# A layer stack with routed experts on one core: overflow blocks ahead of expert 28, products of ones during the routing, and up weights in four transfers

## The reference, cut to what matters

```python
def hier_moe(u, ...):                       # u: 264 x 1024
    g_sel = argmax(x @ w_group + b_group)   # one of 4 groups
    vals, idx = top_k(inner logits of that group, 2)
    gate = softmax(vals) * g_w
    expert_id = g_sel * 8 + idx             # two of 32 experts for a token
    return moe_experts(x, expert_id, gate, w1, w3, w2)
...
    hmid = silu(xblk @ w1[e]) * (xblk @ w3[e])    # 1024 -> 512, twice
    return hmid @ w2[e]                           # 512 -> 1024
...
h = h + hier_moe(rmsnorm(h), ...)
h = h + sigmoid(rmsnorm(h) @ w_gate + b_gate) * (p_i @ w_proj)    # ple
```

## Time and profile before

| | us |
|---|---|
| median of 3 runs (1632.49 to 1643.6) | 1632.73 |
| profiled execution, its own time | 1640.69 |
| its span | 1638.9 |
| TensorE busy (mean granted clock 0.835) | 1212.1 |
| DVE busy | 505.1 |
| ACT busy | 264.8 |

### The profile page before, as it was taken

One profiled execution on the slowest core, in us unless ns is written; L12 is line 12 of the kernel. 1 busy time (PEld: TensorE's weight loads), 2 busy tenths in 40 slices (PEclk: granted clock), 3 DMA queues, 4 the chain that ended last, 5 costly groups with the idle time before them and its releaser, 6 DMA issues. The chain is left out here.

```text
span 1638.9 us, 23206 instructions
## 1 busy us (share of the span) xinstructions
PE 1212.1 (74%) x10112; PEld 784.2 (48%) x10112; DVE 505.1 (31%) x1337; ACT 264.8 (16%) x643; POOL 58.9 (4%) x46
## 2 busy tenths in 40 slices
PE   6978697865766756479898897979675776766577
PEld 4846454433433433247675554745443443433355
DVE  2783512112111111143575663141111112111133
ACT  1262221100100000001224431012010000000011
POOL 0430000000000000000200100000000000000000
PEclk9989788877877877769999996959887887787788
DMA  5853259999999999915213432719999999999820
GB/s 158 278 206 133 103 239 419 420 420 422 420 419 422 422 419 419 416 73 174 103 45 137 153 137 103 280 54 381 419 419 423 421 419 419 422 421 419 353 104 27
DMA packets 91279, 477.03 MB, mean 291 GB/s; under 512 B 21676, under 2 KB 32841, under 8 KB 73230
## 3 DMA queue, kind: packets, MB, share of 16 engines
q1 hardware_dynamic: 89188, 456.35, 68.9%
q0 software_dynamic: 1792, 18.88, 3.1%
q10 hardware_dynamic: 186, 0.20, 0.0%
HBM read 473.37 MB, written 2.49 MB: 290 GB/s over the span
## 5 line engine op out<-in xcount | busy, mean ns | idle before, releaser
L878 PE MATMUL ps<-area,hiddenT 128*32 128x256 f32 x2112 | 214.3, 575 | 287.7 <-issue 279.9
L878 PEld LDWEIGHTS ps<-area,hiddenT 128*32 128x32 f32 x2112 | 97.7, 155 | 376.8 <-issue 368.3
L1417 DVE COPY y<-ps 32x256 f32<-32x256 f32 x128 | 53.3, 417 | 534.8 <-PE ps L878 526.3
L868 PE MATMUL ps<-area,uT 128*32 128x256 f32 x2176 | 145.4, 425 | 4.0 <-issue 1.7
L1151 PE MATMUL ps<-sel,u_rows 128*128 128x256 f32 (+3 forms) x480 | 136.9, 417 | 10.4 <-DVE sel L1123 10.4
L868 PE MATMUL ps<-area,xsT 128*32 128x256 f32 x2048 | 131.6, 412 | 0.0
L1371 ACT COPY y<-ps 32x256 f32<-32x256 f32 x128 | 46.7, 365 | 485.1 <-PE ps L878 484.1
L868 PEld LDWEIGHTS ps<-area,uT 128*32 128x32 f32 x2176 | 85.8, 126 | 64.5 <-issue 32.3
L1151 PEld LDWEIGHTS ps<-sel,u_rows 128*128 128x128 f32 (+1 forms) x480 | 85.3, 214 | 55.0 <-issue 49.9
L868 PEld LDWEIGHTS ps<-area,xsT 128*32 128x32 f32 x2048 | 80.2, 123 | 53.4 <-issue 21.9
L1276 PE MATMUL ps<-share,y 128*128 128x264 f32 x256 | 77.5, 429 | 13.7 <-DVE y L1417 9.9
(11 more groups left out here) (324 smaller groups left out, 1260.1 us busy)
## 6 DMA issues: line engine op xcount, KB each, us to landing
area<-in_w_exp_gate_dram SPq DMA_DIRECT2D x66, 2048.0 KB, 27.0
area<-in_w_exp_up_dram SPq DMA_DIRECT2D x66, 2048.0 KB, 30.7
area<-in_w_exp_down_dram SPq DMA_DIRECT2D x66, 2048.0 KB, 26.2
area<-in_conv_w_in_dram SPq DMA_DIRECT2D x8, 1024.0 KB, 12.8
area<-in_w_ple_gate_dram SPq DMA_DIRECT2D x2, 4096.0 KB, 17.8
area<-in_conv_w_out_dram SPq DMA_DIRECT2D x1, 4096.0 KB, 19.2
area<-in_w_o_dram SPq DMA_DIRECT2D x1, 4096.0 KB, 13.2
area<-in_w_uq_dram SPq DMA_DIRECT2D x3, 768.0 KB, 10.1
```

The lines of the kernel that those rows point to most:

```text
L868: last = pe.matmul(s.ps[SLOT * j:SLOT * (j + 1), bank, 0:2 * P].rearrange("p (a f) -> p a f", a=2), xT[:, k, :], up[:, :, k, j * P:(j + 1) ...
L878: last = pe.matmul(s.ps[SLOT * g:SLOT * (g + 1), bank, 0:q], hidden[:, SLOT * j:SLOT * (j + 1)], down[:, j, g * q:(g + 1) * q], start=(j = ...
L1417: last = V.tensor_copy(y[a:a + SLOT, (e // PER) % 2, g * q4:(g + 1) * q4], s.ps[SLOT * g:SLOT * (g + 1), 3 + e % 2, 0:q4])
```

## The change

Overflow blocks run ahead of expert 28 (`CUT`) instead of behind expert 31, on all engines, and are added to the tokens four at a time. The loop of loads is written anew: up to expert 27 its order is as before, and from there on it is up e, down e in place of up e+1, down e. Overflow block q uses the slots of expert 28 + q, so the loads of expert 28 wait for the blocks (`ov.up`, `ov.down`). `PLE_SLOT` becomes 2, the slot of expert 29, and the attention's buffers change rooms accordingly. Eight and twelve products of ones stand on TensorE in the routing (`busy`); their result is not used. Each half of the contraction of gate and up is a transfer of its own, 1 MB each, and a half has its own semaphore, for which TensorE waits in the midst of the up products. The register load of the number of overflow blocks moves from the start of the stage to expert 28.

```diff
-PLE_SLOT = 1
+PLE_SLOT = 2
+CUT = E - PER
...
-def load_up(engine, s, io, slot, index, sem):
+def load_up(engine, s, io, slot, index, sems):
     up = up_view(s, slot)
-    for a, w in enumerate((io["w_exp_gate"], io["w_exp_up"])):
-        src = w.rearrange("l e (p k) f -> (l e) p (k f)", p=P)[bass.ds(index, 1)]
-        engine.dma_start(up[:, a].rearrange("p k f -> p (k f)"), src.rearrange("a p n -> (a p) n"))\
-            .then_inc(sem, 16)
+    for half, sem in enumerate(sems):
+        k = slice(DC // 2 * half, DC // 2 * (half + 1))
+        for a, w in enumerate((io["w_exp_gate"], io["w_exp_up"])):
+            src = w.rearrange("l e (p k) f -> (l e) p k f", p=P)[bass.ds(index, 1), :, k]
+            engine.dma_start(up[:, a, k], src.rearrange("a p k f -> (a p) k f")).then_inc(sem, 16)
...
+        def busy(pe, n):
+            for k in range(n):
+                pe.matmul(s.ps[:, 3, 0:T], s.ones[:], s.uT[:, k % DC, :], start=True, stop=True)
...
+                busy(pe, 8)
                 pe.wait_ge(s.gated.sem, s.gated.at(2))
...
                 pe.wait_ge(s.turned_out_act.sem, on_act)
+                busy(pe, 12)
                 pe.wait_ge(s.sel_ready.sem, s.sel_ready.at(1))
...
+        def blocks_of(engine, n, block, quad_begins=None, quad_ends=None, after=None):
+            def chain(q):
+                with engine.If(n > q):
+                    block(q)
+                    if (q + 1) % PER:
+                        chain(q + 1)
+                    if after is not None:
+                        after(q)
+            def quad(b):
+                with engine.If(n > PER * b):
+                    if quad_begins is not None:
+                        quad_begins(b)
+                    chain(PER * b)
+                    if quad_ends is not None:
+                        quad_ends(b)
+                    if b + 1 < MAX_OVER // PER:
+                        quad(b + 1)
+            quad(0)
...
+                def up(e):
+                    sp.wait_ge(s.up_done.sem, s.up_done.at(e - UPS + 1))
+                    load_up(sp, s, io, e, e + layer * E, [half.sem for half in s.up_in[e % UPS]])
...
+                for e in range(UPS, CUT):
+                    up(e)
+                    down(e - 1)
                 n = overflow(sp)
...
+                with sp.If(n > 0):
+                    more_up(0)
+                down(CUT - 1)
+                blocks_of(sp, n, more, after=lambda q: sp.wait_ge(ov.up, q + 1))
+                up(CUT)
+                blocks_of(sp, n, lambda q: sp.wait_ge(ov.down, q + 1))
+                down(CUT)
+                for e in range(CUT + 1, E):
+                    up(e)
+                    down(e)
+                sp.wait_ge(s.up_done.sem, s.up_done.at(E - UPS + 1))
                 load_ple_gate(sp, s, io, layer)
...
+                def combine_more(b):
+                    pe.wait_ge(ov.g_ready, b + 1)
                     for c in range(DC):
...
+                        pe.matmul(s.ps[:, 6 + c % 2, 0:T], y[:, 1, c * P:(c + 1) * P], more_share[:, 0, :],
                                   start=True, stop=True).then_inc(ov.comb_mm, 1)
...
-                n = overflow(pe)
                 for e in range(E):
...
+                    if e == CUT:
+                        blocks_of(pe, overflow(pe), more, quad_ends=combine_more,
+                                  after=lambda q: pe.wait_ge(ov.y_ready, q + 1))
+                    def ready(k):
+                        if k % (DC // 2) == 0:
+                            half = k // (DC // 2)
+                            pe.wait_ge(s.up_in[e % UPS][half].sem, up_at(e)[half])
...
-                further(pe, more, n)
                 for c in range(DC):
                     combine(quads - 1, c)
```

More of the change, by code:

```diff
@@ L241, in setup_state @@
         ov.sel_half, ov.sel_ready = sem("ov_sel_half", layer), sem("ov_sel_ready", layer)
-        ov.xs_mm, ov.xs_out, ov.g_half = sem("ov_xs_mm", layer), sem("ov_xs_out", layer), sem("ov_g_half", layer)
-        ov.up_in = [sem(f"ov_up_in{i}", layer) for i in range(UPS)]
+        ov.xs_mm, ov.xs_out = sem("ov_xs_mm", layer), sem("ov_xs_out", layer)
+        ov.g_half, ov.g_ready = sem("ov_g_half", layer), sem("ov_g_ready", layer)
+        ov.up_in = [[sem(f"ov_up_in{i}_{half}", layer) for half in range(2)] for i in range(UPS)]
         ov.down_in = [sem(f"ov_down_in{i}", layer) for i in range(DOWNS)]
         s.over_sems.append(ov)
-    s.up_in = [Count(ctx, nc, f"up_in{i}") for i in range(UPS)]
+    s.up_in = [[Count(ctx, nc, f"up_in{i}_{half}") for half in range(2)] for i in range(UPS)]
     s.down_in = [Count(ctx, nc, f"down_in{i}") for i in range(DOWNS)]
@@ L854, in first_up @@
 def first_up(sp, s, io, layer, n):
-    load_up(sp, s, io, n, layer * E + n, s.up_in[n].sem)
+    load_up(sp, s, io, n, layer * E + n, [half.sem for half in s.up_in[n]])
 def first_down(sp, s, io, layer, n):
@@ L929, in _ @@
             def _(sp):
-                first_up(sp, s, io, layer, 2 - layer)
+                first_up(sp, s, io, layer, 2)
             @block.tensor
@@ L1193, in fill_at, with over_xsT @@
             return (i + 1, f) if 0 <= f < pairs else None
+        def over_xsT(g):
+            return xsT[0 if g == GROUPS else 1]
         def up_at(n):
-            return s.up_in[n % UPS].at(32 * (n // UPS + 1))
+            return [half.at(32 * (n // UPS + 1)) for half in s.up_in[n % UPS]]
         def down_at(n):
@@ L1216, in more_up @@
                     if q < UPS:
[L1217 removed]
+                        sp.wait_ge(s.up_done.sem, s.up_done.at(CUT - UPS + q + 1))
                     else:
                         sp.wait_ge(ov.up, q - UPS + 1)
[L1220 removed]
+                    load_up(sp, s, io, CUT + q, e + layer * E, ov.up_in[(CUT + q) % UPS])
                 def more_down(q):
@@ L1234, in more, with down @@
                     more_down(q)
-                n = overflow(sp)
[L1237 to L1256, removed]
+                def up(e):
+                    sp.wait_ge(s.up_done.sem, s.up_done.at(e - UPS + 1))
+                    load_up(sp, s, io, e, e + layer * E, [half.sem for half in s.up_in[e % UPS]])
+                def down(e):
+                    sp.wait_ge(s.down_done.sem, s.down_done.at(e - DOWNS + 1))
+                    load_down(sp, s, io, e, e + layer * E, s.down_in[e % DOWNS].sem)
+                for e in range(UPS, CUT):
+                    up(e)
+                    down(e - 1)
+                n = overflow(sp)
+                with sp.If(n > 0):
[9 more added lines that the diff above has]
+                sp.wait_ge(s.up_done.sem, s.up_done.at(E - UPS + 1))
                 load_ple_gate(sp, s, io, layer)
@@ L1419, in copy_out, with weigh_more @@
                     last.then_inc(s.y_dve.sem, 1)
+                def weigh_more(b):
+                    halves = weigh(nc, m, P, more_share, col(s, "over_of")[:, b:b + 1])
+                    next(halves).then_inc(ov.g_half, 1)
+                    dve.wait_ge(ov.g_half, b + 1)
+                    next(halves).then_inc(ov.g_ready, 1)
                 def more(q):
@@ L1460, in _ @@
                     quad = e // PER
+                    if e == CUT:
+                        blocks_of(dve, overflow(dve), more, weigh_more, add_more)
                     dve.wait_ge(s.acted.sem, s.acted.at(e + 1))
@@ L1483, in experts_stage @@
         for k in range(UPS):
-            s.up_in[k].ended(32 * len(range(k, E, UPS)))
+            for half in s.up_in[k]:
+                half.ended(32 * len(range(k, E, UPS)))
         for k in range(DOWNS):
```

92 lines of the change are left out of this document (40 added, 52 removed).

## The result

The changed kernel takes **1591.06 us** (1589.04 to 1591.81, four runs), the kernel before 1635.10 beside it (1632.49 to 1643.60, four runs): a ratio of 0.972, 95% interval 0.9681 to 0.9759. That is 44 us less where 37 were forecast. The profiled execution has a span of 1589.6 us.

The account below looks back on a forecast made before the run. Transfers at 420 GB/s were taken to bound the expert stage, leaving routing, tail and byte rate to win. Terms -18.2 + 11.4 - 18.9 - 11.5 = -37.2 took 1632.7 to 1596 us, range 1587 to 1608 (chance 0.58).

Parts of the forecast that it names:

- Products of ones, -18: Routing, both layers: filler products keep TensorE's clock high through dispatch and expert 0; with the register load, -9.1 us per layer.
- expert 0 gains 2.7: Start of the expert stage: expert 0's up products take 3.64 us at 2.4 GHz instead of 6.31.
- The 1.2 us of delay: Routing: the twelve products end at 199.0, so the dispatch starts 1.2 us later than 197.8.
- Four transfers, +11: Expert plateaus: 8 KB pieces flow at 417 GB/s, 0.19 us more per expert over 60 loads.
- the rate of 402: Plateaus: 4 KB pieces taken to flow at 402 GB/s, from 410 at a share of 1.02.
- Overflow, layer 0, -19: Layer 0's blocks and end: 7.5 us of empty queue plus a 12.1 us tail replace 38.5 us.
- The step up to block 1's up products: Ahead of expert 28, layer 0: bytes end at 35.6 us, block 1's up products at 37.8, counted from down 26.
- Tail, layer 1, -11.5: End of layer 1, without blocks: from down 31's landing to the ple stage 12.1 us instead of 23.6.
- Clock: Rival, routing: the twelve products do not bring the high clock through the dispatch; 1615 or 1628 us, chance 0.17.
- Pieces as 4 KB: Rival, plateaus: 8 KB pieces flow no faster than 4 KB ones; 1619 us, chance 0.10.
- Free halves: Rival, plateaus: 8 KB pieces flow as fast as 16 KB ones; 1585 us, chance 0.10.
- The wall at expert 28: Rival, layer 0: SP loads expert 28 only when the blocks are fully done; 1637 us, chance 0.05.

Follow-up runs that it names:

- two_transfers: The changed kernel with gate and up weights as two transfers again (16 KB pieces), up products waiting for both: 1585.29 us.
- eight_transfers: The changed kernel with each half of the up weights cut in two again, eight transfers per expert in 4 KB pieces: 1609.24 us.
- best_down: The changed kernel with two up transfers, expert 28's up load waiting for block 0 only, six products ahead of the router, down weights in 16 KB pieces: 1578.19 us.
- before_ones: The kernel before with only the 20 products of ones per layer added in the routing: 1612.57 us.
- no_ones: The changed kernel without its 20 products of ones in the routing: 1605.92 us.
- early_loads: The changed kernel with up 28, down 28 and up 29 each waiting only for blocks whose rooms they take, in a third walk: 1581.35 us.

## Why the prediction was right

The sign and the range held, and each mechanism was at work: 1596 forecast, 1591 measured; by the stretches 38.2 us for a sum of 37.2. That the sums agree to 1 us is luck: the routing gave 14.2 for 18.2, the experts 24.0 for 19.0. The terms, one by one:

- **Products of ones, -18.** Alone on the kernel before they gave 9.2 and 9.6 us in the routing, for 8.6 without the register load; in the profiled execution of the changed kernel the routing gave 7.1 in each layer, because the router product took 6.70 us and not 5.44, and expert 0 ran part of its 5.33 us at 0.50 (granted clock) where the step "expert 0 gains 2.7" had it at 2.4 GHz throughout. In two_transfers that step holds (3.66). The 1.2 us of delay did not come: the 12 products end (191.77) about when `sel` is ready, since the last turns ahead of them, now at the full clock, take 1.03 us and not 1.87. The gone register load is worth 0.85 in layer 0 (idle 1.72 to 0.87) and 0.68 in layer 1, not 0.5.
- **Four transfers, +11.** They cost 0.14 us per expert (6.29 MB at 416 instead of 420 GB/s), 8.4 for 60; between the two kernels the experts differ by 4.2 + 3.3. Sign and mechanism were right; the term was mis-sized (0.19 per expert). The step that was off is the rate of 402, which is 410 divided by a share of 1.02: in eight_transfers a queue full of 4 KB pieces delivers 409 at a share of 1.03, so the division took away rate that is really there. With 425 and 409 the same working gives 0.13. The longer windows, 425.5 (all 16 KB) and 408.5 (all 4 KB, both means over the two layers), fit a fixed cost of a piece: the measured 416 asks for 419.9 at 8 KB, by (2/3)/419.9 + (1/3)/408.5, and a third of the step from 16 to 4 KB gives 419.7. The traces also show the cost itself: from 300 to 550 us a packet of 4, 8 or 16 KB takes 163, 315 or 617 ns on average, about 151 ns for each 4 KB and 12 for the packet. Two smaller things lie in the 4.2 + 3.3 as well: the dip ahead of expert 28, 7.5 us in two_transfers, costs 1.4 more in the changed kernel, and the halves buy some 2.8 at the ends of the layers, which the forecast put at nothing: from the landing of down 31 to the ple stage it is 10.0 and 9.9 us with them, 11.6 and 11.0 in two_transfers. The Trainium skill, page DMA: Bandwidth & Descriptors, section Specifications, has line rate from 512 bytes on; the trace disagrees, with 409, 416, 420 and 425 for pieces that all lie far above; the length of a piece is all that best_down changes in its transfers.
- **Overflow, layer 0, -19.** The place alone gave 20.7. In the changed kernel 8.9 us of transfer are missing ahead of expert 28 (7.5 forecast). The step up to block 1's up products held: the last bytes flow until 625.2 (the share is 0.33 from 624.5 to 625.0, 0.06 in the next half microsecond, then 0.00), and these products end 2.6 us later, at 627.8 (2.2 forecast). SP's branch took 2.9 (5.3 forecast). Two parts were not in the forecast: from 620.5 to 624.5 the share is only about 0.5, which with the rest of the window 620 to 625 costs 2.3 us, and some 1.1 us pass between SP's load and a full queue. The new tail is 10.0 us from the landing of down 31, not 12.1, so the two errors nearly cancel: 8.9 + 10.0 - 38.5 = -19.6.
- **Tail, layer 1, -11.5.** 11.2 alone, with a new tail of 11.2 us from the landing of down 31 (12.1 forecast; 9.9 with the halves). About 4 of it, the stall in the old combine, is not the blocks' own: before_ones loses it without moving them.
- **Rivals.** Clock: the dispatch is at 1.00; no_ones, where it is at 0.50, is 15 us above the changed kernel for the rival's 19 above the forecast. Pieces as 4 KB: the plateaus would run at 409 as in eight_transfers (1609), and run at 416. Free halves: they would run at 420 as in two_transfers (1585). The wall at expert 28: SP did wait for both up products, the size of the rival was far off, since the down products, the additions and TensorE's 6.76 us of "issue" lie under the loads of expert 28.

The sum of the parts, by the medians: -22.3 (products) + 5 (what both gain in the experts of layer 1) - 32.1 (place) + 5.8 (transfers) = -43.6, the 44 measured. In the profiled execution the forecast's -37 came out because the clock's lapse over expert 0 and the router took about what the cheaper pieces and the place gave beyond their terms.

## What to carry to other kernels

Where the transfers bound a stage, price each edit by what it does ahead of the full queue, behind it, and to the bytes in it. Work in the middle was free here while TensorE kept some slack, and splitting a load for an early start cost more than it bought (8.4 against 2.8 us), since over most of the stage nobody could use the start. When an engine that issues loads waits for "all of it", look which part holds the room of the next load: one changed condition was worth 9 us here. Filler products held TensorE's clock through the waits here (1.00 over the dispatch with them, 0.50 without); count their passes, so that they end with the wait.

## What the runs showed of the hardware that I had not expected

- A moving operand with a stride of four columns halves TensorE's rate: 7.5 against 3.64 us for the same 64 passes at 2.4 GHz.
- The stall behind a branch is not a constant: 0.4, 2.9 and 5.5 us for SP at the blocks (and 0.8 in two_transfers at the wait where the changed kernel shows 2.9), and TensorE's 3.75 in the tail of layer 1 went when products were added to the routing, hundreds of us earlier. The Trainium skill, page Runtime: NRT & Kernel Launch, section Instruction fetch mechanics, has such a fetch behind a taken branch; the traces agree that engines stand still there, though they do not tell the fetch from other causes, and show that the size has to be measured in each build.
- The same router product took 3.75, 5.09, 5.44 or 6.70 us in different executions, all behind the same 2.94 us of idle time (early_loads has 5.44 in layer 0 and 3.75 in layer 1): a step that rests on the clock behind an idle time needs a range.
